# A hybrid S5 and latent-attention trunk: tokens in order of place, another start of each layer, and merges pair by pair

## The reference, cut to what matters

```
for l in range(2):
    mod = silu(c) @ w_ada[l] + b_ada[l]            # sh1, sc1, g1, sh2, sc2, g2
    h = rms_norm(x, norm1_g[l]) * (1 + sc1) + sh1
    u, cq_in, ckv_in, kr_in, gate_a, gate_b = split(h @ w_in[l])
    #  512   256    128     32     1024    1024 columns
    y_a = s5_mixer(u) @ w_a_out[l]                 # state space of 32 groups x 64 states, gelu, GLU
    y_b = mla_mixer(cq_in, ckv_in, kr_in) @ w_b_out[l]   # 8 heads, rotary key, position mask
    merged = sigmoid(gate_a) * y_a + sigmoid(gate_b) * y_b
    x = x + g1 * (merged @ w_out[l])
    h = rms_norm(x, norm2_g[l]) * (1 + sc2) + sh2
    x = x + g2 * ((silu(h @ w_gate[l]) * (h @ w_up[l])) @ w_down[l])
return rms_norm(x, final_g)
```

## Time and profile before

| | us |
|---|---|
| median of three runs | 3251.06 (3249.01 to 3251.24) |
| profiled execution | 3254.23 |
| its span | 3252.1 |
| granted TensorE clock over the span | 0.986 of full |
| TensorE busy | 3122.6 (96%) |
| VectorE busy | 1618.7 (50%) |
| ScalarE busy | 1033.3 (32%) |
| GpSimd busy | 1015.8 (31%) |
| span less TensorE's busy time | 129.5 |

### The profile page before, as it was taken

How to read it: one execution, slowest core, us unless ns; L and a number is a source line. 1 busy time by engine, 2 the same in 40 slices (tenths; PEclk the granted TensorE clock), 3 DMA queues, 4 the chain that set the end, 5 groups by cost and what they waited for, 6 DMA issues and landing times.

```text
span 3252.1 us, 38091 instructions
## 1 busy us (share of the span) xinstructions
PE 3122.6 (96%) x15392; PEld 2648.8 (81%) x15392; DVE 1618.7 (50%) x1987; ACT 1033.3 (32%) x1474; POOL 1015.8 (31%) x582
## 2 busy tenths in 40 slices
PE   5999999999999999999989999999999999999998
PEld 4888879978878888888878888898787788888886
DVE  8897547765242233233279782787543222223224
ACT  3323357762231111111142333677313211111112
POOL 4465322232322222222246651223223222222223
PEclk9999989999999999999999999999999999999999
DMA  6444410014321222211134452001241111111111
GB/s 254 149 156 143 138 32 15 21 49 136 123 72 59 65 71 62 62 59 52 46 136 147 155 165 73 10 21 43 88 161 39 52 46 46 52 46 50 49 46 71
DMA packets 250213, 265.05 MB, mean 82 GB/s; under 512 B 34753, under 2 KB 204865, under 8 KB 248770
## 3 DMA queue, kind: packets, MB, share of 16 engines
q1 hardware_dynamic: 242848, 221.85, 22.1%
q10 hardware_dynamic: 7202, 40.90, 3.4%
HBM read 219.64 MB, written 43.06 MB: 81 GB/s over the span
## 4 chain that ended last, share of the span: by engine, by line
PE 80%; DVE 8%; issue 4%; ACT 3%; POOL 2%; DMA 1%; SPq 0%; DVEq 0%; POOLq 0%; ACTq 0%
PE ps L546 21%; PE ps L548 21%; PE ps L549 21%; PE ps L1339 3%; PE ps L1320 2%; PE ps L1325 2%; PE ps L1324 2%; PE ps L1359 2%; PE ps L1360 2%; PE ps L1158 1%; PE ps L1170 1%; DVE x_sb L2436 1%; DVE silu L2418 1%; POOL sq_sum L876 1%; POOL wlo L530 1%
## 5 line engine op out<-in xcount | busy, mean ns | idle before, releaser
L530 POOL TENSOR_TENSOR wlo<-raw,whi 128x1024 fp32r<-128x1024 f32 (+4 forms) x294 | 564.8, 1930 | 1871.4 <-ACT whi L522 1870.5
L522 ACT ACTIVATE whi<-raw 128x1024 fp32r<-128x1024 f32 (+4 forms) x294 | 247.1, 862 | 1638.6 <-PE ps L549 1584.5
L546 PE MATMUL ps<-h_hi,whi 128*128 128x512 f32 x2048 | 658.1, 397 | 33.7 <-DVE h_lo L2050 17.9
L548 PE MATMUL ps<-h_lo,whi 128*128 128x512 f32 x2048 | 648.2, 393 | 0.0
L549 PE MATMUL ps<-h_hi,wlo 128*128 128x512 f32 x2048 | 646.6, 392 | 0.0
L546 PEld LDWEIGHTS ps<-h_hi,whi 128*128 128x128 f32 x2048 | 383.3, 190 | 118.2 <-DVE h_lo L2050 16.9
L549 PEld LDWEIGHTS ps<-h_hi,wlo 128*128 128x128 f32 x2048 | 388.0, 189 | 82.8
L548 PEld LDWEIGHTS ps<-h_lo,whi 128*128 128x128 f32 x2048 | 388.5, 190 | 81.2
L2418 DVE TENSOR_TENSOR silu<-silu,ps 128x1024 f32<-128x1024 f32 x44 | 53.7, 1221 | 769.5 <-PE ps L549 760.3
L2436 DVE SCALAR_TENSOR_TENSOR x_sb<-ps,mod,x_sb 128x1024 f32<-128x1024 f32 x160 | 203.3, 1280 | 178.0 <-PE ps L549 178.0
L546 PE MATMUL ps<-hid_hi,whi 128*128 128x512 f32 x704 | 224.8, 393 | 9.5 <-DVE x_sb L2436 9.5
(11 more groups left out here) (273 smaller groups left out, 4944.4 us busy)
## 6 DMA issues: line engine op xcount, KB each, us to landing
ada_raw<-in_w_ada SPq DMA_DIRECT2D x64, 512.0 KB, 4.4
raw<-in_w_in SPq DMA_DIRECT2D x100, 256.0 KB, 3.4
raw<-in_w_gate SPq DMA_DIRECT2D x88, 256.0 KB, 3.2
raw<-in_w_up SPq DMA_DIRECT2D x88, 256.0 KB, 3.2
raw<-in_w_down SPq DMA_DIRECT2D x88, 256.0 KB, 2.8
gate_scratch<-gst ACTq DMA_DIRECT2D x32, 512.0 KB, 3.4
gl<-gate_scratch SPq DMA_DIRECT2D x32, 512.0 KB, 4.2
xs_scratch<-x_sb ACTq DMA_DIRECT2D x2, 4096.0 KB, 12.3
```

The source lines that it names most:

```text
L522: last = act.activation(dst(whi[:, s, :]), src(raw[:, s, :]), ACT.Copy)
L530: last = pool.tensor_tensor(dst(wlo[:, s, :]), src(raw[:, s, :]), dst(whi[:, s, :].bitcast(F32)), ALU.subtract)
L546: pe.matmul(o, w_h, x_h, start=first, stop=False)
L548: pe.matmul(o, w_h, x_l, start=False, stop=False)
```

## The change

- **Token order.** The host passes tokens in the order 0, 8, 16, ..., 1, 9, 17, ... (`chunk_order`) and turns the result back (`token_order`). Positions follow. The u products' stationary operand and the copy to `yt_q` are contiguous.
- **Start.** `w_first` and PE's one-column products are gone. DVE makes both first vectors by 16 row sums from a ring of four rows (`ada_rows`); rope tables come after the sixth, the first reciprocal and two masks after the eleventh, `wlo` of units 0 and 1 after the 13th and 15th. PE sums the squares of layer 0 itself (64 matmuls of one column) in place of POOL's 14 additions. Six mask rows move behind the h phase of layer 0. The store of masks and tables moves into the gate loop.
- **h and u.** `U_PRE` is gone, and gate tiles 0 and 1 run whole in their place. h comes in the order (0,0-4), (1,0-4), (0,5), (1,5), ... PE runs u in two passes over k 0 to 3 (steps 0 to 3, then 4 to 7), then k 4 to 7 with all steps.
- **S5.** POOL splits up to gate tile 1 ahead of the matrices; batch 0 has no splits between. In layer 0 the list of parts stands four halves in, not two (`S5_LAG`).
- **Latents.** Other banks; `yt_ev` is waited for before `U_KR` and not before the second cq unit, which now waits for `toe_ready` and `y_gelu`. DVE makes `k_lo` of head 0.
- **End of the attention.** The last two GLU k are two steps later. The last row scale is stored and brought back in two parts, with merge loads 0 and 1 between. POOL splits merge unit 0 before the last head's norm. PE's and POOL's merges are unrolled, and tile 0 waits pair by pair.

The diff, cut to its core:

```diff
+def chunk_order(v):
+    return v.reshape(*v.shape[:-1], -1, 8).swapaxes(-1, -2).reshape(v.shape)
+def token_order(v):
+    return v.reshape(*v.shape[:-1], 8, -1).swapaxes(-1, -2).reshape(v.shape)
...
+        S5_LAG = (4,) + (2,) * (DEPTH - 1)
-        U_STEPS = (1, 2, 3, 4, 5, 6, 0, 7)
-        Y_STEPS = (STEPS - 4, STEPS - 2, STEPS, STEPS + 1)
+        U_STEPS = (1, 2, 3, 4, 0, 5, 6, 7)
+        U_BANK = (7, 0, 1, 2, 3, 4, 5, 6)
+        U_FIRST = 4
+        H_ORDER = [(0, k) for k in range(5)] + [(1, k) for k in range(5)] + [(t, k) for k in range(5, KT) for t in range(2)]
+        Y_STEPS = (STEPS - 4, STEPS - 2, STEPS + 2, STEPS + 3)
...
@@ sync @@
+                if l == 0:
+                    for n in range(2 * KT):
+                        if n == 8:
+                            for t in range(2):
+                                load_unit(sp, l, U_U + t, u_unit(t))
+                        if n >= 4:
+                            sp.wait_ge(rows_used.sem, n - 3)
+                        k, m = divmod(n, 2)
+                        sp.dma_start(ada_rows[:, n % 4, :], w_ada[0][m * D + k * P:m * D + (k + 1) * P, :])\
+                            .then_inc(rows_loaded[n % 4].sem, 16)
...
                 for t in range(2 * KT + 4):
+                    if t == 2:
+                        spill_tables()
...
-                row_scales(PAIRS - 1, 1)
+                scales_out(PAIRS - 1, 1)
...
                 merge_unit(0)
                 merge_unit(1)
+                scales_back(PAIRS - 1, 1)
@@ gpsimd @@
-            for k in range(1, KT):
-                for t in range(2):
-                    add_squares(0, 0, t, k)
...
-                for n in range(U_U, U_GATE + 1):
+                for n in range(U_U + 2, U_GATE + 2):
                     split_lo(pool, l, n)
...
                     inputs()
-                    split_lo(pool, l, U_GATE + 2 * b + 1)
+                    if b:
+                        split_lo(pool, l, U_GATE + 2 * b + 1)
                     outputs()
...
-                wait(pool, q_ready, l, 2)
-                rotary_lo(0)
...
+                wait(pool, o_ready, l, 2 * PAIRS - 1)
+                split_lo(pool, l, U_MERGE)
                 head_norm(PAIRS - 1, 1)
...
-                with pool.Fori(0, 4) as i:
-                    for j in range(2):
-                        split_lo(pool, l, U_MERGE + j, i)
+                for n in range(1, KT):
+                    split_lo(pool, l, U_MERGE + n)
@@ tensor @@
+            for half in range(2):
+                if half:
+                    wait(pe, std_ready, 0, 1)
+                for k in range(KT):
+                    pe.wait_ge(sq_ready[half].sem, k + 1)
+                    for t in range(4):
+                        last = pe.matmul(ps[:, 6, 4 * half + t:4 * half + t + 1],
+                                         sq_ring[:, 2 * half + k % 2, t * P:(t + 1) * P], mean_col[:, :],
+                                         start=(k == 0 and t == 0), stop=(k == KT - 1), skip_group_check=True)
...
+                    if half and k == 3:
+                        norm_scale(0, 0)
...
+                def u_products(k, steps):
...
+                    for j in steps:
+                        bank = U_BANK[j]
+                        x_h, x_l = h_hi[:, k, j * NC:(j + 1) * NC], h_lo[:, k, j * NC:(j + 1) * NC]
+                        pe.matmul(ps[:, bank, :], x_h, w_h, start=(k == 0), stop=False)
+                        pe.matmul(ps[:, bank, :], x_h, w_l, start=False, stop=False)
+                        last = pe.matmul(ps[:, bank, :], x_l, w_h, start=False, stop=(k == KT - 1))
...
+                for k in range(U_FIRST):
+                    wait(pe, h_ready, l, h_number(0, k) + 1)
+                    u_products(k, range(0, 4))
+                    if k == 1 and l:
+                        mean_squares(l, 1)
+                    if k == 2:
+                        norm_scale(l, 1)
+                for k in range(U_FIRST):
+                    wait(pe, h_ready, l, h_number(1, k) + 1)
+                    last = u_products(k, range(4, CH))
+                for k in range(U_FIRST, KT):
+                    wait(pe, h_ready, l, h_number(1, k) + 1)
+                    last = u_products(k, U_STEPS)
...
-                    b, part = divmod(h - 2, 4)
+                    b, part = divmod(h - S5_LAG[l], 4)
...
-                wait(pe, yt_ev, l, 8)
+                wait(pe, toe_ready, l, 8)
+                wait(pe, y_gelu, l, 8)
                 latent_unit(U_CQ + 1)
...
-                wait(pe, toe_ready, l, 8)
-                wait(pe, y_gelu, l, 8)
+                wait(pe, yt_ev, l, 8)
                 latent_unit(U_KR)
...
+                for t in range(KT):
+                    j = t % 2
+                    unit_ready(pe, l, U_MERGE + t)
+                    wait(pe, mg_free, l, t - 1)
+                    if t == 0:
+                        wait(pe, glu_sig, l, 2)
+                    for k in range(PAIRS):
+                        if t == 0:
+                            wait(pe, o_ready, l, 2 * (k + 1))
+                        tile_products(pe, j, 4 * j + 2, o_hi, o_lo, [(4 + k, k)], first=(k == 0), last=(k == PAIRS - 1))
+                    if t == 0:
+                        wait(pe, yg_ready, l, 4)
+                    end = tile_products(pe, j, 4 * j, yg_hi, yg_lo, [(k, k) for k in range(4)])
@@ scalar @@
+                hidden_hi(l, 0, 3)
                 norm_std(l, 1)
+                hidden_hi(l, 0, 4)
                 norm_rows(l, 1)
-                for t in range(2):
-                    hidden_hi(l, 1, t)
-                    wait(act, unit_used, l, U_PRE + t + 1)
-                    act.activation(gst[:, t, 0:HALF], ps[:, (7, 0)[t], :], ACT.Sigmoid).then_inc(pre_act.sem, 1)
-                    split_hi(act, l, U_U + t)
-                for k in range(2, KT):
-                    hidden_hi(l, 1, k)
+                for o, k in H_ORDER[5:]:
+                    hidden_hi(l, o, k)
+                    if (o, k) == (0, 5):
+                        split_hi(act, l, U_U + 2)
+                if l == 0:
+                    for k in range(KT):
+                        mask_block(k)
                 wait(act, s5_loaded, l, 16)
                 act.activation(sm[:, S_DT, :], ldt, ACT.Exp).then_inc(s5_act.sem, 1)
-                split_hi(act, l, U_U + 2)
+                split_hi(act, l, U_U + 3)
@@ vector @@
+            for n in range(2 * KT):
+                k, m = divmod(n, 2)
+                dve.wait_ge(rows_loaded[n % 4].sem, 16 * (n // 4 + 1))
+                row_products(mod[:, m, k:k + 1], ada_rows[:, n % 4, :], first_c[:, :]).then_inc(rows_used.sem, 1)
+                if n == 5:
+                    rope_tables()
+                if n == 10:
+                    dve.wait_ge(std_ready.sem, 1)
+                    dve.reciprocal(rstd[:, 0, 0:4], std[:, 0, 0:4]).then_inc(rstd_ready.sem, 1)
+                    for t in range(2):
+                        mask_rows(t)
+                if n in (12, 14):
+                    t = n // 2 - 6
+                    wait(dve, w_hi_done, 0, U_U + t + 1)
+                    lo_of(wlo[:, t, :], raw[:, t, :], whi[:, t, :]).then_inc(w_lo_done.sem, 1)
...
+                for o, k in H_ORDER[4:]:
+                    hidden_lo(l, o, k)
+                if l == 0:
+                    for k in range(2, KT):
+                        mask_rows(k)
+                    dve.wait_ge(mask_step.sem, KT)
+                    dve.sem_inc(tables_ready.sem, 1)
...
+                wait(dve, kr_hi_done, l, 1)
+                lo_of(k_lo[64:P, 0, :], kr_t[64:P, 0, :], k_hi[64:P, 0, :]).then_inc(kr_ready[0].sem, 1)
```

More of the change, by code:

```diff
@@ L1009, in _ @@
                 head_lo(PAIRS - 1, 0)
+                wait(pool, o_ready, l, 2 * PAIRS - 1)
+                apart(pool)
+                split_lo(pool, l, U_MERGE)
+                wait(pool, w_lo_done, l, U_MERGE + 1)
+                apart(pool)
                 head_norm(PAIRS - 1, 1)
@@ L1053, in _ @@
             pe.wait_ge(pool_const.sem, 2)
-            pe.wait_ge(act_const.sem, 1)
-            for k in range(KT):
-                pe.wait_ge(first_loaded[k % 2].sem, 16 * (k // 2 + 1))
-                for n in range(KT):
-                    last = pe.matmul(ps[:, 0, n:n + 1], first_raw[:, k % 2, n * P:(n + 1) * P], c_act[:, k:k + 1],
-                                     start=(k == 0 and n == 0), stop=(k == KT - 1), skip_group_check=True)
-                last.then_inc(first_mm.sem, 1)
             def mean_squares(l, o):
@@ L1216, in _ @@
                     unit_ready(pe, l, U_GATE + t)
-                    wait(pe, z_act, l, 2 * t + 1 if t < 2 else 7 + t)
+                    wait(pe, z_act, l, 2 * t + 2 if t < 2 else 7 + t)
                     for half in range(2):
-                        if t < 2:
-                            for k in range(4 * half, 4 * half + 4):
```

(12 more changed lines are left out.)

328 lines of the change are left out of this document (137 added, 191 removed).

## The result

The changed kernel takes 3227.61 us (median of four runs, 3225.63 to 3231.59) against 3250.03 us for the kernel before: a ratio of 0.9932, 95% interval 0.9919 to 0.9944, so 22.4 us less. Its profiled execution took 3231.59 us, the slowest of the four, with a span of 3229.8, 22.3 under the span before.

The account below looks back on a forecast made before the run. TensorE was taken as the bound, busy 3122.6 of 3252.1 us, with winnable time in many short waits. Terms summed to 33.5 us off 3254.2, giving 3220.7, or 3218 at the median; range 3198 to 3234, the forecast's own 3209 to 3228.

Parts of the forecast that it names:

- The start: Program start to layer 0's gate tile 2: earlier first h product and S5 chain, tile 2 at 149.5; 4.5 us gained.
- Layer 1: Hand-over from layer 1's S5 chain: VectorE starts the chain 2.45 us earlier; 4.7 us gained after clock loss.
- Token order: u products of both layers: contiguous loads save 3.1 us per layer, counted at nothing because the S5 chain ends later.
- yt_q term: Latents: moving TensorE's wait on yt_q one unit later removes gap and slow products; 4.4 and 5.5 us gained.
- First scores: Start of attention: VectorE instead of GpSimd makes k_lo, removing that wait; 2.7 and, in layer 1, 3.7 us gained.
- The o_un wait: Attention's end: the last wait on o_un falls from 1.5 to 0.5 us; 1.0 us gained a layer.
- what I had set beside the sum: First scores: if VectorE's k_lo and GpSimd's q_lo pair shut each other out, 0.6 us less gain per layer.
- The merges: From the GLU's end into the merge: tile 0 goes pair by pair with one split; 3.6 and 2.4 us gained.
- what ends last is the chain ..., or 7.0: Merges: yg follows the GLU's end by a 7.0 us chain of sigmoid, hi, lo, multiply, hi, lo.
- the case of gains given back: Rival across all hand-overs: each uncovers the next wait, losing a third of the sum; 3230 to 3240 us, chance 0.10.
- The slower rival: Layer 0 gates: longer lag makes GpSimd's inputs late, 5.9 us at each of seven batches; 3259 us, chance 0.05.

Follow-up runs that it names:

- e3: Changed kernel with ScalarE doing the S5 chain's first exponential and splitting u unit 3 ahead of layer 0's mask blocks: 3230.92 us.
- e12: Changed kernel with all mask rows and mask blocks of layer 0 written ahead of h, none behind the h phase: 3233.07 us.
- e1: Changed kernel with GpSimd splitting gate tile 2 ahead of the S5 matrices, later gate splits one earlier, and layer 1's lag four halves too: 3204.49 us.
- e6: Changed kernel with TensorE again waiting for yt_q ahead of the second cq unit, beside the two waits now there: 3234.71 us.
- e2: Changed kernel with ScalarE rounding the last head's output one GLU tile later: 3227.97 us.
- e9: Changed kernel with merge tile 0 waiting for all heads at once and GpSimd splitting its unit behind the last head's norm, as before: 3230.27 us.
- e8: Changed kernel with tokens ordered so u's stationary operand is read at a stride of four columns and yt_q copied in strides: 3230.27 us.

## Why the prediction was right, and where it was too large

The forecast was 3218 with a range from 3198 to 3234; measured 3227.61. The sign, the places and most mechanisms held; the sum was 33.5 and 22.4 came.

- **The start.** First product at 55.85 (57.2 forecast), chain at 96.71 (98.9), matrices at 130.81 (133.4), tile 2 at 148.05 (149.5) with 12.45 idle (11). That the S5 chain and not TensorE sets the start, which the sum rested on, is shown by e3 and e12, and e1 shows that it does so through POOL's order. With 5.45 for 4.5 the term was good. The split ahead of gate tile 2 took 3.32 and not the 2.4 that I had.
- **Layer 1** was put too low: the chain starts 5.0 us earlier against its layer (13.76 at 1688.65, less the 8.72 brought along; DVE's row at 1674.89), not 2.45, so 7.27 for 4.7.
- **Token order**: 188 ns loads and no time from them, as said. The yt_q term (4.46 and 5.53 for 4.4 and 5.5) was right, and for the reason given: e6 shows 9.1 of its 10.0 us to be the moved wait's. The faster copy, which I had named without a price, has the other 0.9.
- **First scores**: k_lo's wait went from 1.97 to 0.63, and 1.5 of it came back on v_st, a wait that the later start had hidden. That step failed in both layers: scores and attention 5.2 for 8.4. The o_un wait did not fall at all; it is still 1.5 twice. What is left of the k_lo wait is what I had set beside the sum (0.6 less in each layer): VectorE's k_lo runs beside POOL's q_lo pair (440.56 to 444.00) and takes 1.99 us, where a TENSOR_TENSOR of that shape at 440.38 takes 1.22; it ends at 445.09, just ahead of the scores at 445.23. The row of 2.41 that I named for it is a TENSOR_SCALAR with one tensor input, and so no case of two inputs.

```profile
443.10 1.99 DVE L1964 TENSOR_TENSOR k_lo<-kr_t,k_hi 64x1024 fp32r<-64x1024 f32 x1 [0.18 <-ACT k_hi L1570]
```

- **The merges** are the term that was wrong: -1.7 for +6.0. The step that failed is "what ends last is the chain ..., or 7.0". I let the chain begin at the GLU's end. With two buffers the fourth sigmoid has to wait for the second tile's low part, and that one is late because ScalarE's queue stands 5.04 us ahead of the last head's rounding. (e2 takes this stand away, and GpSimd's work beside VectorE's takes most of its place.) ScalarE of the changed kernel:

```profile
714.99 1.06 ACT L1570 ACTIVATE o_hi<-o_un 64x1024 fp32r<-64x1024 f32 x1 [5.04 <-POOL o_un L987]
716.08 1.12 ACT L1866 ACTIVATE glu_s<-ps,pcol 128x1024 f32<-128x1024 f32 x1
717.09 1.06 ACT L1570 ACTIVATE yg_hi<-glu_s 128x1024 fp32r<-128x1024 f32 x1
719.71 1.12 ACT L1866 ACTIVATE glu_s<-ps,pcol 128x1024 f32<-128x1024 f32 x1 [1.56 <-DVE yg_lo L1964]
```

```profile
726.64 1.05 PE L552 MATMUL ps<-yg_hi,whi 128*128 128x512 f32 x2 [4.31 <-DVE yg_lo L1964]
```

  The sigmoid starts at 719.71 and not at 716.89. From there the chain takes the 6.9 us that its terms add up to, so its length was right and its start was 2.8 us off; yg comes 9.75 behind the GLU, as against 10.64. Of the 5.6 us of products behind the 4.31 us gap the first eight run at the lower clock (two take 1.05 and not 0.62), and the whole takes 7.32. That is the second part of the term that I left out. In layer 0 the kernel before paid the same for the clock, in its o half behind the gap of 3.48; in layer 1 its gaps of 2.55 and 1.09 brought no slow products, and now the gap of 3.25 does:

```profile
732.15 1.05 PE L548 MATMUL ps<-o_lo,whi 128*128 128x512 f32 x2
...
2316.60 0.72 PE L546 MATMUL ps<-o_hi,whi 128*128 128x512 f32 x2 [2.55 <-POOL wlo L530]
2317.16 0.63 PE L548 MATMUL ps<-o_lo,whi 128*128 128x512 f32 x2
```

```profile
2299.09 0.73 PE L552 MATMUL ps<-yg_hi,whi 128*128 128x512 f32 x2 [3.25 <-DVE yg_lo L1964]
...
2301.58 1.06 PE L554 MATMUL ps<-yg_lo,whi 128*128 128x512 f32 x2
```

  (The first fence is the kernel before, the second the changed one.) From the GLU's end to the o half of tile 1 layer 0 takes 16.91 for 16.08, all of it the longer gap, and layer 1 15.87 for 14.97: 0.4 us less of gaps and 1.3 more of slow products. So the term turns negative. By e9, undoing the earlier o half changes nothing clear of noise.
- **Losses with no term**: 1.8 behind the latents (lat_sq waits 2.15 for 0.98 in layer 0; in layer 1 the wait is the same and the squares' products take 5.63 for 4.93), 1.7 ahead of the FFN of layer 0, where TensorE meets x_sb's addition for 1.43 us. They are of the kind that the case of gains given back was for, and with the merges and the first scores the shortfall is 11 of 33.5, the third of the sum that this case named. Its time of 3230 to 3240 was not reached: 3227.61 lies 0.4 under the upper end of the forecast's own 3209 to 3228. Some of that is luck, since 14.7 us lost at the first scores, the merges and here (0.3 at the end of layer 1 with them) were met by 3.6 that the start, layer 1 and the latents brought beyond their terms.
- **The slower rival** had the order of waits wrong. The inputs of a batch wait for the Toeplitz products of the batch two before, not of the one before. It did not show: after gate tile 2 no wait on POOL of over a microsecond stands in the gates of layer 0.

Left open: how much of the start's gain comes from POOL no longer adding squares (no run gives them back to it), and what layer 1's gain owes to the order of h, the two passes and the gate tiles one by one.

## What to carry to other kernels

Ahead of a hand-over, ask of each queue what it does while it waits, and put there what another engine will need right behind: a gate split moved ahead of nine instructions, the later ones with it and a longer lag, brought as much as the whole change. When a wait is taken away, price the chain from the last free buffer and not from the last product, and expect that a wait hidden by the late start shows up behind it. Price a gap with the slow products behind it: in e6 a wait of 1.36 us behind one-column products came to 4.0. A gap that can't be closed can be covered by the next tile's independent half.

## What the runs showed of the hardware

- The weight load of a 128x128 fp32r tile takes 188 ns contiguous, 309 to 310 at a stride of four columns and 331 at eight.
- A copy of 128x512 from PSUM on ScalarE takes 600 ns into contiguous columns and 1177 into strides of eight; into strides of four, in e8, 1120.
- A two-input VectorE instruction of 1.22 us beside one of GpSimd took 3.42 us. One split more of 2.44 us on GpSimd beside the S5 chain lengthened it by 2.05 us (e1), one less shortened it by 2.1 (e3).
- Behind a gap of TensorE the granted clock can fall to the lower of its two levels: two products of 128x512 then take 1.05 us in place of 0.62. It did so behind gaps of 3.25 and 4.31 us in the changed kernel, and not behind 2.55 and 1.09 in the kernel before; behind one-column products and a gap of 1.36 it did in e6. The window from 714 to 740 has a mean granted clock of 0.93.
